# The first norm inside the first block's stream, the second norm beside its tail, and a reordered lead-in of the experts

## The chip, the cores and the metric

The kernel runs on one core of one Trainium2 chip. The metric is the time on the device in microseconds (us) of one execution. "Engines" are TensorE (PE, with its weight load PEld), VectorE (DVE), ScalarE (ACT), GpSimd (POOL) and SyncE (SP), which issues most of the DMAs.

## What is computed

Two blocks on 256 tokens of width 2048, float32. The change touches the first block: a norm, an input projection whose columns go to a gated linear attention (GLA, 4 heads) and to a dilated window attention (12 heads), the output projection with the residual, a second norm, and an expert layer.

```python
def rms_norm(x, g):
    y = x * lax.rsqrt(jnp.mean(x * x, axis=-1, keepdims=True) + EPS)
    return y * g
...
    xn = rms_norm(x, norm1_g[l])
    h = xn @ w_in[l]
    qa, ka, va, gdf, gdb, ra, qd, kd, vd = jnp.split(h, split_points, axis=-1)
    oa = gla_mixer(qa, ka, va, gdf, gdb, ra, ...)   # gates: log_sigmoid(gd @ up + bias)
    od = dilated_mixer(qd, kd, vd, ...)
    x = x + concatenate([oa, od]) @ w_out[l]
    x = x + peer_ffn(rms_norm(x, norm2_g[l]), w_query, sub_keys, expert_down, expert_up)
```

`peer_ffn` makes 8 query heads, scores each against two sets of 128 keys, takes the best 16 pairs of each head and gathers their rows of `expert_down` and `expert_up` (8 KB each), 128 rows per token: the dot with the normed token through a gelu, times a softmax gate, weighs the up row.

## The kernel before

**Stream.** `project` (L429) runs a list of weight chunks (`Stream`). A chunk is 2 of the 16 row tiles of a weight (512 KB; the two gate chunks hold 8 each, 288 KB). SP loads it into one of 8 slots once the chunk that was there is used, ACT rounds it (`high`, L466), DVE subtracts (`low`, L487), and TensorE does three matmuls for each tile, high by high, high by low and low by high (L517, L520). ACT and DVE run through the chunks ahead of TensorE as far as the slots allow. Finished blocks are taken out by ACT (L412), or, for the output projection `out1`, added to the residual by DVE (L409) and squared by ACT (L419) for the next norm. The activations have high and low parts too; those of the first block are made inside the stream (L394, L399).

**Beside work.** Everything of the attentions lies in generators that run at ticks (two chunks each, written by hand): `gla_beside` (L636) starts with tick 2, where TensorE multiplies the gates (L690), DVE adds the bias (L822) and ACT and DVE make the log gate (L775 to L827), for which TensorE waits at tick 4 (L694). On SP, ACT and DVE a tick comes 3 ticks (6 chunks) earlier in the chunk count than on TensorE. Within one engine the order of the program is the order of the work.

**First norm.** Ahead of the stream `normalise` (L529) waits for x and for all constants (1505 KB), squares (L561, L580), takes the root (L563), the reciprocal (L586), scales x (L566, L589), turns it on TensorE (L607) and takes it out with the gain (L569, L592). The weights of the first eight chunks are loaded meanwhile.

**Second norm.** The same function runs between the stream and the experts, with the squares' sums from the stream (L578).

**Experts.** `peer` (L1208): queries (L1287), with those of head 0 split by tokens (L1303) and its scores (L1309); DVE sorts (L1475 to L1512); POOL gathers a row for each of 128 tokens (L1459, 2.10 MB) into 4 slots; DVE makes the dot (L1551), ACT gelu, gate and diagonal (L1392 to L1396), TensorE adds (L1318), and frees the slot. 16 units (8 heads by 2 token tiles) of 16 rows each. Queries of heads 0, 1 and 2 come before the first unit, those of 3 to 7 one step per row inside units 1 to 5. `load_query` (L1200) loads 2 MB for each head into one of two rooms.

## Time and profile before

| | us |
|---|---|
| median of 3 runs | 2331.84 (2329.73 to 2332.44) |
| the profiled execution | 2329.87 |
| its span, first to last instruction | 2328.1 |

```profile
span 2328.1 us, 21752 instructions
...
PE 2056.1 (88%) x8141; PEld 1333.8 (57%) x8141; DVE 1299.4 (56%) x2001; ACT 814.3 (35%) x1737; POOL 260.3 (11%) x267
...
PE   6999999997989889977777898899877799999997
...
PEclk9999999999999999989999999999999999999999
DMA  5545556469999999999999999999999656466662
```

The last three lines cut the span into 40 slices of 58 us; a digit is a share in tenths. The first block's stream fills slices 1 to 8, the expert layer slices 8 to 31, where the DMAs are full, and the second block the rest.

### The profile page before, as it was taken

What the parts mean: (1) busy time and instruction counts of PE and PEld (TensorE: products, weight loads), DVE (VectorE), ACT (ScalarE), POOL (GpSimd) and SP (SyncE); (2) the same over time, 40 slices, a digit from 0 to 9 for tenths busy, and PEclk for the clock granted to TensorE, in tenths of its full rate; (3) what the DMA queues carried; (4) which work ended last, traced back from release to release, by engine and by line L of the source; (5) the groups of instructions that cost most, each with busy time, mean ns of one, the idle gap of its engine ahead of it and who ended that gap; (6) DMA issues with size and microseconds to landing.
All of it is one profiled execution on the core that took longest, in us unless ns stands there. A gap on an engine that the chain in (4) does not pass through costs nothing. (4 is left out here: it accounts for less than half of the span.)

```text
span 2328.1 us, 21752 instructions
## 1 busy us (share of the span) xinstructions
PE 2056.1 (88%) x8141; PEld 1333.8 (57%) x8141; DVE 1299.4 (56%) x2001; ACT 814.3 (35%) x1737; POOL 260.3 (11%) x267
## 2 busy tenths in 40 slices
PE   6999999997989889977777898899877799999997
PEld 5878778772444444422323344444322798999886
DVE  5545665445654555545566555556644666475555
ACT  5446564412212212212222322122121655355454
POOL 0000000002121211112112111111211000000000
PEclk9999999999999999989999999999999999999999
DMA  5545556469999999999999999999999656466662
GB/s 211 163 135 164 162 176 209 166 284 429 427 428 428 427 428 427 426 426 414 428 428 428 427 427 424 426 427 425 413 428 405 202 146 187 123 203 200 185 195 80
DMA packets 87513, 729.90 MB, mean 314 GB/s; under 512 B 10192, under 2 KB 10320, under 8 KB 51696
## 3 DMA queue, kind: packets, MB, share of 16 engines
q0 software_dynamic: 36864, 536.89, 54.4%
q1 hardware_dynamic: 50544, 191.63, 25.5%
q8 instruction: 64, 1.05, 0.2%
q14 instruction: 41, 0.34, 0.0%
HBM read 724.28 MB, written 4.19 MB: 313 GB/s over the span
## 5 line engine op out<-in xcount | busy, mean ns | idle before, releaser
L1318 PE MATMUL bank<-ring,work 128*128 128x512 f32 x2048 | 962.9, 614 | 205.9 <-ACT work L1396 202.9
L1551 DVE CUSTOM_DVE_ANT_0 ring<-ring,mix_t 128x2048 f32<-128x2048 f32 x256 | 586.9, 2293 | 551.9 <-DMA ring<-in_peer_rows_dram,work 549.7
L1318 PEld LDWEIGHTS bank<-ring,work 128*128 128x128 f32 x2048 | 374.6, 192 | 726.2 <-issue 380.7
L487 DVE TENSOR_TENSOR ring_r<-ring,ring_r 128x1024 fp32r<-128x1024 f32 (+2 forms) x300 | 334.5, 1145 | 304.5 <-ACT ring_r L466 303.9
L1459 POOL DMA_INDIRECT ring<-in_peer_rows_dram,work x256 | 256.3, 1001 | 1511.8 <-PE bank L1318 965.2
L1392 ACT ACTIVATE work<-work 128x1 f32<-128x1 f32 x256 | 52.4, 205 | 958.9 <-DVE work L1551 958.8
L520 PE MATMUL bank<-ring_r,mix_r 128*128 128x512 f32 (+1 forms) x1184 | 374.6, 391 | 0.0
L466 ACT ACTIVATE ring_r<-ring 128x1024 fp32r<-128x1024 f32 (+2 forms) x300 | 288.5, 992 | 168.4 <-DMA ring<-in_w_out_dram 52.0
L520 PE MATMUL bank<-ring_r,act_r 128*128 128x512 f32 (+1 forms) x736 | 269.1, 387 | 0.0
L520 PEld LDWEIGHTS bank<-ring_r,mix_r 128*128 128x128 f32 x1184 | 220.3, 189 | 42.1 <-issue 1.8
L517 PE MATMUL bank<-mix_r,ring_r 128*128 128x256 f32 (+1 forms) x1216 | 227.4, 289 | 7.7 <-DVE ring_r L487 7.7
L517 PEld LDWEIGHTS bank<-mix_r,ring_r 128*128 128x128 f32 (+1 forms) x1216 | 191.8, 192 | 9.3 <-DVE ring_r L487 8.2
L517 PE MATMUL bank<-act_r,ring_r 128*128 128x256 f32 (+1 forms) x608 | 174.1, 286 | 0.0
L520 PEld LDWEIGHTS bank<-ring_r,act_r 128*128 128x128 f32 x736 | 138.3, 188 | 27.0
L1287 PEld LDWEIGHTS bank<-act_t,h 128*128 128x128 f32 x576 | 109.0, 190 | 60.7 <-issue 51.7
L1287 PE MATMUL bank<-act_t,h 128*128 128x256 f32 x576 | 142.9, 379 | 0.0
L517 PEld LDWEIGHTS bank<-act_r,ring_r 128*128 128x128 f32 (+1 forms) x608 | 116.7, 192 | 0.0
L1396 ACT ACTIVATE work<-const,work 128x128 f32<-128x128 f32 x256 | 103.2, 403 | 8.3
L520 PE MATMUL bank<-ring_r,h_r 128*128 128x512 f32 x288 | 83.2, 394 | 0.9 <-DVE h_r L2612 0.9
L1393 ACT ACTIVATE work<-work 128x1 f32<-128x1 f32 x256 | 76.1, 297 | 8.3
L412 ACT ACTIVATE h<-bank 128x256 f32<-128x256 f32 (+3 forms) x67 | 32.0, 487 | 123.2 <-PE bank L520 89.1
L520 PEld LDWEIGHTS bank<-ring_r,h_r 128*128 128x128 f32 x288 | 53.8, 188 | 12.6 <-DVE h_r L2612 1.3
(372 smaller groups left out, 1252.1 us busy)
## 6 DMA issues: line engine op xcount, KB each, us to landing
ring<-in_w_in_dil_dram SPq DMA_DIRECT2D x72, 512.0 KB, 3.6
ring<-in_w_out_dram SPq DMA_DIRECT2D x64, 512.0 KB, 3.6
ring<-in_w_in_mo_dram SPq DMA_DIRECT2D x48, 384.0 KB, 3.6
h<-in_w_query_dram SPq DMA_DIRECT2D x8, 2048.0 KB, 11.8
ring<-in_w_in_gla_dram SPq DMA_DIRECT2D x24, 512.0 KB, 3.6
ring<-in_w_in_ml_oz_dram SPq DMA_DIRECT2D x24, 512.0 KB, 3.8
h<-in_xa_wkv_dram SPq DMA_DIRECT2D x4, 2048.0 KB, 21.3
ring<-in_w_in_lru_dram SPq DMA_DIRECT2D x16, 512.0 KB, 3.6
```

Source lines behind the costliest of these rows:

```text
L412: eng.activation(job.dest(c.b, g), src, ACT.Copy).then_inc(k.group_out[False], 1)
L466: act.activation(high(c), raw(c), ACT.Copy).then_inc(k.weights_high, 1)
L487: dve.tensor_tensor(low(c), raw(c), plain(high(c)), ALU.subtract).then_inc(k.weights_low, 1)
L517: m = pe.matmul(bank[0:job.m, 0:T], w[:, q, g * job.m:(g + 1) * job.m], a[:, q, :], start=start, stop=stop)
L520: m = pe.matmul(bank[:, 0:job.cols], a[:, q, g * P:(g + 1) * P], w[:, q, :], start=start, stop=stop)
L1287: m = pe.matmul(bank[:, f * T:(f + 1) * T], a, w, start=kc == 0, stop=kc == KC - 1)
L1318: m = pe.matmul(B[c][:, :], diag[:, d % 2, :], slots[:, d % DEPTH, 1, c * 512:(c + 1) * 512], start=first, stop=last)
L1392: step(act.activation(gelu[:, p, j:j + 1], dots[:, p, j:j + 1], ACT.Gelu_apprx_tanh))
L1393: step(act.activation(coef[:, p, j:j + 1], gelu[:, p, j:j + 1], ACT.Copy, scale=gates[:, p, j:j + 1]))
L1396: act.activation(diag[:, d % 2, :], k.c("ident"), ACT.Copy, scale=coef[:, p, j:j + 1]).then_inc(diag_ready, 1)
L1459: pool.indirect_dma_start(slots[:, d % DEPTH, :, :].rearrange("p a b -> p (a b)"), None, ins["peer_rows"], bass.IndirectOffsetOnAxis(ap=ro ...
L1551: dve.tensor_tensor_reduce(row, row, xn[:, t, :], 1.0, 0.0, ALU.mult, ALU.add, dots[:, p, j:j + 1]) \
```

## The change

- The first `normalise` goes. `norm1_beside` does its work at the head of the stream: a first part of the constants (identity and the gains, 208 of the columns) and x in four pieces of 512 columns are loaded first; TensorE turns x unscaled, two pieces at tick 0 and two at tick 0.5, that is behind the first gate chunk; ACT takes out the high part with the gain and DVE the low part; the squares follow at ticks -1.5 to 0, mean and root at 0.5, the reciprocal at 1. The root `rstd1` is applied where the blocks are taken out (ACT's scale) and, for the gates, in the bias step. The other constants are loaded at tick -1, and `gla_beside` waits for them. L394 and L399 fall away.
- The parts of `out1`'s activations change places: high in `mix_r`, low in `act_r` and `mix_r`.
- The second `normalise` goes. `norm2_beside` turns the unscaled residual, quarters 0 and 1 inside the stream's last chunks, quarters 2 and 3 behind it; ACT and DVE take out two pieces of each quarter; the root goes to the scores' take-outs (`staged`, `later`).
- In `peer` there are three rooms for queries (the third in `mem_kv` and the gain's place), each load is two DMAs of 1 MB, head 2 is loaded once the gain is used and its query moves into unit 0; score 0 and score 1 come after 6 of 16 matmuls of the next group; `xn` is made by one product of x, root and gain.

The diff, cut:

```diff
+                scale = 1.0 if job.scale is None else job.scale[:, g:g + 1]
+                eng.activation(job.dest(c.b, g), src, ACT.Copy, scale=scale).then_inc(k.group_out[False], 1)
...
+def norm1_beside(k, mem, beside, stream, name="norm1"):
+    B, gain, ins = k.banks, k.c("norm1_g"), k.ins
+    x_hi, x_lo = shaped(k.mix_r[:, :], KC, T), shaped(k.act_r[:, :], KC, T)
+    junk = shaped(k.h[:, 0:NT * D], NT, 4, 512)
+    ident_in, const_in, x_turned, x_high, x_low, squared_act, squared_dve, own, meaned, rooted, inverted = (
+        k.sem(f"{name}_{n}") for n in ("ident_in", "const_in", "x_turned", "x_high", "x_low", "squared_act", "squared_dve",
+                                       "own", "meaned", "rooted", "inverted"))
+    x_in = [k.sem(f"{name}_x_in{b}") for b in range(4)]
+    cols = lambda b: slice(b * 512, (b + 1) * 512)
+    turn_at = lambda kc: B[(4, 5, 6, 7, 2, 3, 4, 5)[kc // 2]][:, kc % 2 * T:(kc % 2 + 1) * T]
+    TICKS = (-AHEAD, -AHEAD, -AHEAD + 0.5, -AHEAD + 0.5)
+    SQUARES = [-AHEAD + 1.5 + 0.5 * b for b in range(4)]
+    x_rows = ins["x"].rearrange("(t p) d -> p t d", p=P)
+    def load(sp):
+        yield -AHEAD
+        sp.dma_start(k.const[:, 0:FIRST_CONSTS], ins["consts"][:, 0:FIRST_CONSTS]).then_inc(ident_in, 16)
+        for b in range(4):
+            if b == 2:
+                yield TICKS[b]
+            sp.dma_start(k.x3[:, :, cols(b)], x_rows[:, :, cols(b)]).then_inc(x_in[b], 16)
+        yield -AHEAD + 2
+        sp.dma_start(k.const[:, FIRST_CONSTS:], ins["consts"][:, FIRST_CONSTS:]).then_inc(const_in, 16)
+    def tensor(pe):
+        yield 0
+        pe.wait_ge(ident_in, 16)
+        for b in range(4):
+            if b == 2:
+                yield 0.5
+            pe.wait_ge(x_in[b], 16)
+            if b == 3:
+                pe.wait_ge(x_low, 4)
+            for kc in range(4 * b, 4 * b + 4):
+                for t in range(NT):
+                    m = pe.transpose(turn_at(kc)[:, t * P:(t + 1) * P], k.x3[:, t, kc * P:(kc + 1) * P], k.c("ident"))
+                if kc % 2:
+                    m.then_inc(x_turned, 1)
+    def scalar(act):
+        for b, tick in enumerate(TICKS):
+            yield tick
+            if b == 0:
+                act.wait_ge(ident_in, 16)
+            for kc in range(4 * b, 4 * b + 4):
+                act.wait_ge(x_turned, kc // 2 + 1)
+                act.activation(x_hi[:, kc, :], turn_at(kc), ACT.Copy, scale=gain[:, kc:kc + 1]).then_inc(x_high, 1)
+        for b, tick in enumerate(SQUARES):
+            yield tick
+            act.wait_ge(x_in[b], 16)
+            act.activation(junk[:, 0, b, :], k.x3[:, 0, cols(b)], ACT.Square, accum_out=k.sums3[:, 0, b:b + 1]).then_inc(squared_act, 1)
+        yield 0.5
+        act.wait_ge(meaned, 1)
+        act.activation(mem.sd1, mem.ms1, ACT.Sqrt).then_inc(rooted, 1)
+        yield 3
+        act.wait_ge(inverted, 1)
+    def vector(dve):
+        for b, tick in enumerate(TICKS):
+            yield tick
+            for kc in range(4 * b, 4 * b + 4):
+                dve.wait_ge(x_high, kc // 2 * 2 + 2)
+                dve.scalar_tensor_tensor(x_lo[:, kc, :], turn_at(kc), gain[:, kc:kc + 1], x_hi[:, kc, :].bitcast(F32),
+                                         ALU.mult, ALU.subtract).then_inc(x_low, 1)
+        for b, tick in enumerate(SQUARES):
+            yield tick
+            dve.wait_ge(x_in[b], 16)
+            x = k.x3[:, 1, cols(b)]
+            dve.tensor_tensor_reduce(junk[:, 1, b, :], x, x, 1.0, 0.0, ALU.mult, ALU.add, k.sums3[:, 1, b:b + 1]).then_inc(squared_dve, 1)
+        yield 0.5
+        dve.wait_ge(squared_act, 4)
+        dve.wait_ge(squared_dve, 4)
+        dve.tensor_reduce(mem.sd1, k.sums3, AX.X, ALU.add).then_inc(own, 1)
+        dve.wait_ge(own, 1)
+        dve.tensor_scalar(mem.ms1, mem.sd1, 1.0 / D, EPS, ALU.mult, ALU.add).then_inc(meaned, 1)
+        yield 1
+        dve.wait_ge(rooted, 1)
+        dve.reciprocal(mem.rstd1, mem.sd1).then_inc(inverted, 1)
+        dve.wait_ge(inverted, 1)
+    beside.load.append(load)
+    beside.tensor.append(tensor)
+    beside.scalar.append(scalar)
+    beside.vector.append(vector)
+    for n in range(2):
+        stream.chunks[n].needs = [(x_low, KC // 2 * (n + 1))]
+    return const_in
...
-            step(dve.tensor_tensor(la[:, t, :], B[4 + t][:, :], bias, ALU.add))
+            step(dve.scalar_tensor_tensor(la[:, t, :], B[4 + t][:, :], mem.rstd1[:, t:t + 1], bias, ALU.mult, ALU.add))
...
+def norm2_beside(k, mem, beside, stream, out1, rstd, name="norm2"):
+    B, gain = k.banks, k.c("norm2_g")
+    turned, taken_act, taken_dve, own, meaned, rooted, inverted = (k.sem(f"{name}_{n}") for n in (
+        "turned", "taken_act", "taken_dve", "own", "meaned", "rooted", "inverted"))
+    first, end = stream.at(out1, 2), len(stream.chunks)
+    TICKS = [(first + 5) / PER_TICK, (first + 6) / PER_TICK, end / PER_TICK, end / PER_TICK + 1]
+    turn_at = lambda kc: B[kc // 2 % 4][:, kc % 2 * T:(kc % 2 + 1) * T]
+    def tensor(pe):
+        for b, tick in enumerate(TICKS):
+            yield tick
+            pe.wait_ge(*stream.out(out1, b))
+            if b >= 2:
+                pe.wait_ge(taken_act, 2 * (b - 1))
+                pe.wait_ge(taken_dve, 2 * (b - 1))
+            for kc in range(4 * b, 4 * b + 4):
+                for t in range(NT):
+                    m = pe.transpose(turn_at(kc)[:, t * P:(t + 1) * P], k.x3[:, t, kc * P:(kc + 1) * P], k.c("ident"))
+                if kc % 2:
+                    m.then_inc(turned, 1)
+    def scalar(act):
+        for b, tick in enumerate(TICKS):
+            yield tick
+            if b == 3:
+                act.wait_ge(meaned, 1)
+                act.activation(mem.sd, mem.ms, ACT.Sqrt).then_inc(rooted, 1)
+            act.wait_ge(turned, 2 * b + 1)
+            for kc in (4 * b, 4 * b + 1):
+                act.activation(k.act3[:, kc, :], turn_at(kc), ACT.Copy, scale=gain[:, kc:kc + 1]).then_inc(taken_act, 1)
+    def vector(dve):
+        for b, tick in enumerate(TICKS):
+            yield tick
+            dve.wait_ge(turned, 2 * b + 2)
+            for kc in (4 * b + 2, 4 * b + 3):
+                dve.tensor_scalar(k.act3[:, kc, :], turn_at(kc), gain[:, kc:kc + 1], None, ALU.mult).then_inc(taken_dve, 1)
+            if b == 2:
+                dve.wait_ge(k.squared, NT * 4)
+                dve.tensor_reduce(mem.sd, k.sums3, AX.X, ALU.add).then_inc(own, 1)
+                dve.wait_ge(own, 1)
+                dve.tensor_scalar(mem.ms, mem.sd, 1.0 / D, EPS, ALU.mult, ALU.add).then_inc(meaned, 1)
+        dve.wait_ge(rooted, 1)
+        dve.reciprocal(rstd, mem.sd).then_inc(inverted, 1)
+    beside.tensor.append(tensor)
+    beside.scalar.append(scalar)
+    beside.vector.append(vector)
...
+    gla.scale = dil.scale = mem.rstd1
...
-    def load_x(sp, arrived):
-        sp.dma_start(k.x3, ins["x"].rearrange("(t p) d -> p t d", p=P)).then_inc(arrived, 16)
-        sp.dma_start(k.const[:, :], ins["consts"]).then_inc(arrived, 16)
-    normalise(k, "norm1", k.x3, k.c("norm1_g"), k.act3, load=load_x, upcoming=stream)
     beside = Beside()
-    gla_turned, gla_low = gla_beside(k, mem, beside, stream.out(gates, 0), *(stream.out(gla, b) for b in range(3)))
+    const_in = norm1_beside(k, mem, beside, stream)
...
+def query_room(head):
+    if head < 3:
+        return head, 1
+    return (0, (head + 1) // 2) if head % 2 else (1, head // 2)
+def query_before(head):
+    return head - 3 if head < 5 else head - 2
...
-            for head in range(2, PEER_H):
-                sp.wait_ge(query_done, head - 1)
+            sp.wait_ge(gained, NT)
+            load_query(sp, k, 2, query_in)
+            for head in range(3, PEER_H):
+                sp.wait_ge(query_done, query_before(head) + 1)
                 load_query(sp, k, head, query_in)
...
-            for f in range(2):
-                first_tokens(f, 0, B[4 + f][:, 0:P]).then_inc(first_query, 1)
+            pe.wait_ge(*query_there(0))
+            first_tokens(0, 0, B[4][:, 0:P]).then_inc(first_query, 1)
+            first_tokens(1, 0, B[5][:, 0:P], range(6))
             pe.wait_ge(keys_in, 16)
             first_score(0)
-            first_tokens(0, 1, B[0][:, 0:P])
+            first_tokens(1, 0, B[5][:, 0:P], range(6, KC)).then_inc(first_query, 1)
+            first_tokens(0, 1, B[0][:, 0:P], range(6))
             first_score(1)
+            first_tokens(0, 1, B[0][:, 0:P], range(6, KC))
...
-            query(2, 0, range(KC))
-            score(2, 0)
             for n in range(UNITS):
                 for j in range(K):
-                    if 0 < n < PEER_H - 2:
+                    if n < PEER_H - 2:
                         query(n + 2, n % 2, [j])
...
-                dve.tensor_tensor(xn[:, t, :], xn[:, t, :], gain, ALU.mult).then_inc(gained, 1)
+                dve.scalar_tensor_tensor(xn[:, t, :], k.x3[:, t, :], rstd[:, t:t + 1], gain, ALU.mult, ALU.mult).then_inc(gained, 1)
```

## Rows read from the trace of the kernel before

**Rows 1.** Busy us by stretch; last three: granted clock, DMA share, GB/s.
```profile
350.00:400.00 50.00, 50.00 (x231) 41.59 (x230) 28.86 (x41) 25.43 (x43) 0.00 (x0) 1.00 0.56 174
700.00:800.00 100.00, 89.50 (x243) 43.63 (x242) 53.48 (x80) 25.06 (x71) 20.71 (x20) 1.00 1.01 428
```

**Rows 2.** Timeline of the start: start us, busy us, instruction, [idle before <-releaser].
```profile
12.04 2.29 DVE L580 CUSTOM_DVE_ANT_0 mix_t<-x_res 128x2048 f32<-128x2048 f32 x1 [12.04 <-DMA const<-in_consts_dram]
...
16.35 5.39 PE L607 MATMUL bank<-const,mix_t 128*128 128x128 f32 x32 [16.35 <-ACT mix_t L566]
17.20 0.46 ACT L569 ACTIVATE act_t<-bank,const 128x256 f32<-128x256 f32 x1
...
25.60 0.46 PE L517 MATMUL bank<-mix_r,ring_r 128*72 128x256 f32 x2 [3.86 <-DVE ring_r L487]
...
29.53 4.63 DVE L487 TENSOR_TENSOR ring_r<-ring,ring_r 128x1024 fp32r<-128x1024 f32 x4
...
32.83 0.63 PE L520 MATMUL bank<-ring_r,mix_r 128*128 128x512 f32 x2
```

**Rows 3.** DMA issues, 0 to 50 us: KB each, us from issue to landing.
```profile
x_res<-in_x_dram SPq DMA_DIRECT2D x1, 2048.0 KB, 7.7
```

**Rows 4.** Busy time by stretch, at the start (last three: clock, DMA share, GB/s).
```profile
4.00:6.00 2.00, 0.00 (x0) 0.00 (x0) 0.00 (x0) 0.00 (x0) 0.00 (x0) 1.00 1.00 422
...
27.00:28.00 1.00, 1.00 (x6) 1.00 (x5) 1.00 (x2) 1.00 (x2) 0.00 (x0) 0.50 0.00 0
```

**Rows 5.** Timeline of the gate chain, of eight transposes, and of the second norm.
```profile
39.61 0.69 DVE L822 TENSOR_TENSOR x_res<-bank,mem_kv 128x512 f32<-128x512 f32 x1 [0.59 <-PE bank L690]
...
43.53 1.28 ACT L777 ACT_TABLE_LOAD   x1
44.83 1.06 ACT L777 ACTIVATE x_res<-x_res 128x1024 f32<-128x1024 f32 x1
...
49.15 1.22 DVE L827 SCALAR_TENSOR_TENSOR x_res<-x_res 128x1024 f32<-128x1024 f32 x1
...
51.30 0.59 PE L694 MATMUL bank<-x_res,const 128*128 128x256 f32 x2
...
186.96 1.09 PE L1011 MATMUL bank<-const,h 128*128 128x128 f32 x8 [0.75 <-DVE h L967]
...
451.46 1.30 DVE L409 TENSOR_TENSOR x_res<-bank,x_res 128x512 f32<-128x512 f32 x2 [1.42 <-PE bank L520]
...
453.33 0.19 ACT L419 ACTIVATION_READ_ACCUMULATOR work<-x_res 128x1 f32 x1
...
460.42 1.36 DVE L592 TENSOR_SCALAR act_t<-bank,const 128x256 f32<-128x256 f32 x3 [0.30 <-PE bank L607]
...
462.10 7.38 PE L1303 MATMUL bank<-act_t,h 128*128 128x128 f32 x64 [0.84 <-PEq L545]
```

**Rows 6.** Timeline of the experts' lead-in, and one gather of the steady stretch.
```profile
473.11 0.39 PE L1309 MATMUL bank<-h 128*128 128x128 f32 x2
...
477.11 31.05 SPq L1204 DMA_DIRECT2D h<-in_w_query_dram  x3
...
478.10 13.98 PE L1287 MATMUL bank<-act_t,h 128*128 128x256 f32 x64
...
483.34 1.08 POOL L1459 DMA_INDIRECT ring<-in_peer_rows_dram,work  x1 [458.99 <-DVE work L1512]
...
511.32 15.70 PE L1318 MATMUL bank<-ring,work 128*128 128x512 f32 x32 [1.68 <-ACT work L1396]
...
517.49 0.94 POOL L1459 DMA_INDIRECT ring<-in_peer_rows_dram,work  x1 [29.34 <-PE bank L1318]
...
559.23 0.94 POOL L1459 DMA_INDIRECT ring<-in_peer_rows_dram,work  x1 [3.95 <-PE bank L1318]
```

**Rows 7.** Busy time by stretch, around the first gathers.
```profile
480.00:485.00 5.00, 5.00 (x24) 4.39 (x24) 2.32 (x6) 0.00 (x0) 1.36 (x2) 1.00 0.76 321
...
515.00:520.00 5.00, 5.00 (x14) 2.13 (x13) 4.96 (x7) 0.96 (x4) 0.94 (x1) 1.00 0.29 66
```

More of the change, by code:

```diff
@@ L109 @@
 GATE_M = 72
+FIRST_CONSTS = P + 5 * KC
 class Area:
@@ L526, in _, with normalise @@
             rest(len(chunks) // PER_TICK)
-def normalise(k, name, src3, gain, dst3, load=None, upcoming=None, late=None, summed=False):
+def normalise(k, name, src3, gain, dst3, upcoming=None, late=None):
     nc = k.nc
@@ L547, in _ @@
         def _(sp):
-            if load is not None:
-                load(sp, arrived)
             if upcoming is not None:
@@ L596, in _ @@
         def _(pe):
-            if load is not None:
-                pe.wait_ge(arrived, 32)
             for kc in range(KC):
@@ L628, in __init__ @@
         self.top, self.den = area.take(DIL_H, NT), area.take(2, DIL_H, NT)
+        self.ms1, self.sd1, self.rstd1 = (area.take(NT) for _ in range(3))
         area = Area(x[:, :])
@@ L1299, in score, with first_tokens @@
                 m.then_inc(scored, 1)
-            def first_tokens(f, t, bank):
-                for kc in range(KC):
-                    m = pe.matmul(bank, wq[:, 0, kc, f * PEER_K:(f + 1) * PEER_K], k.act3[:, kc, t * P:(t + 1) * P],
+            def first_tokens(f, t, bank, part=range(KC)):
+                for kc in part:
+                    m = pe.matmul(bank, wq(0, kc)[:, f * PEER_K:(f + 1) * PEER_K], k.act3[:, kc, t * P:(t + 1) * P],
                                   start=kc == 0, stop=kc == KC - 1)
```

112 lines of the change are left out of this document (62 added, 50 removed).

## The prediction

> **What bounds the kernel now.** I read first the stretches by busy time and granted clock, to see which engine has no room. In the first block's stream TensorE is busy 50 of 50 us at the full clock, with the DMAs at half load [rows 1]: there every microsecond by which the stream starts earlier should arrive at its end. In the expert stage it is the other way round: the DMAs are at 1.01 and 428 GB/s while TensorE is busy 89.5 of 100 [rows 1], and the 2.10 MB of one gather take 4.9 us at that rate. There the time is that of the bytes, plus the holes in which the DMAs idle. So four places count: the norm ahead of the stream, the seam between stream and expert stage, the lead-in to the first gathers, and the bytes and holes behind it. The timelines of these are what I read next.
>
> **Part 1, the first norm.** Before, nothing starts until x and all constants have landed at 12.04 [rows 2], though x's own transfer, the first one, issued at about 0.75, took 7.7 us [rows 3]; the first gate matmul starts at 25.60 and the first one of the tok chunks at 32.83 [rows 2]. I work the change out in the order in which each engine has it. The DMAs run at 422 GB/s from 4 us on [rows 4], and x as a whole was in by 8.45 [rows 3]; counted back at that rate, the small constants and the first quarter of x, 0.63 MB together, are in at about 4.9, the second quarter at 6.2, the rest by 9.4. TensorE turns the first quarter. Before, the first copy followed the first transpose by 0.85 us with two transposes [rows 2]; with four, 1.1: 6.1. ACT takes 8 pieces at 0.45 each (0.46 alone [rows 2]): 9.7. It rounds the gate weights and DVE subtracts (0.67 and 0.75): the first gate chunk can start at 11.1. The other half's transposes stand behind that chunk in TensorE's order. The granted clock was 0.50 (1.2 GHz) in the stretch from 27 us [rows 4], about 1 us after TensorE had come back from a wait of 3.86 us, and full again at about 30. Here the wait is 3.5 us, so I take the chunk slow. Sixteen steps took 7.1 us with that drop [rows 2]; eight take 2.8 fast and 4.2 with one. That gives 15.3. Eight more copies from 16.0 end at 19.6, rounding and subtraction at 21.0, the second gate chunk with a drop again at 25.2 (22.6 at the full clock). So TensorE comes to the tok chunks 7.6 us earlier (up to 10).
>
> Not all of that stays. The squares on ACT (0.62 each) and DVE (0.65 each), the mean and the root now lie in the same programs as the rounding of the weights. DVE subtracts a chunk in 1.14 (four took 4.63 [rows 2]). It begins chunk 2 at 21.1; eight chunks (9.1), four squares (2.6) and the steps between the engines for mean, root and reciprocal (2.3) put it at 35.1 for the gate logits, which TensorE has ready at 32.8. Before, DVE began them at 39.61, the log gate was ready at 50.37, and TensorE came for it at 51.30, 0.9 us later [rows 5]. From logits to log gate are 10.8 us, two weight chunks among them: 35.1 + 10.8 = 45.9. TensorE, coming at 43.7, waits 2.2 us. **What is late next** is thus this chain over DVE and ACT. Gain at that point 51.3 - 46.0 = 5.3; with one more drop of the clock behind the wait 3.6; with no drop anywhere 6.7. I take **4.5 us**, ends 1 and 9 (no row shows x in pieces of 2 KB a partition; a later landing goes one to one).
>
> The root needs a table on ACT where before that was loaded in the empty start. A load takes 1.28 us, and the next ACTIVATE starts 0.02 behind it [rows 5]; it falls in the wait for the mean and costs at most 1. The Trainium skill ("ScalarE: Activation LUTs", What ACT_TABLE_LOAD costs) adds a drain of 1.38 us to each load. By it the log gate would come about 1 us later. The trace shows no such drain.
>
> The scale at the take-outs lengthens ACT copies, where ACT is busy 25.4 of 50 us [rows 1]: nothing. The second part of the constants, 1.4 MB, lands at about 15 and its first reader comes at 30: nothing. SP's four small loads no longer stand behind the norm: nothing, their readers are later.
>
> **Part 2, the second norm.** Before, TensorE ends the stream at 452.0, the last take-out at 452.76, the squares at 453.52, the norm's last take-out at 461.78, and the queries start at 462.10 [rows 5]. After, half of the 32 transposes lie inside the stream, which TensorE bounds; eight in a row took 1.09 us with their tail [rows 5], 0.117 apart: +1.9 us. Sixteen are left behind it: TensorE turns the third quarter until 453.0, the fourth until 454.0; ACT ends its squares, copies two pieces until 454.4, takes the root at 454.85 and copies two more until 455.95; DVE ends with the reciprocal at 456.0. With the 0.32 us that the change of programs took, the queries start at 456.3: 5.8 earlier, less 1.9 is 3.9. But TensorE then sat idle for 2.3 us. Waits of 3.86 and 1.68 us [rows 2, 6] were followed by a drop of the clock, one of 0.84 us [rows 5] was not; a drop costs about 1.7 (half of 3.4). I take it: **2.2 us**, ends 1 and 4.
>
> **Part 3, the lead-in.** Call the queries' start S (462.10 before). Score 1 starts at S+11.0 and the first gather at S+21.24 [rows 6]. After, 16 + 6 matmuls, score 0, 10 + 6 matmuls and then score 1: 38 steps of 0.231 and 0.22, S+9.0. The first gather is issued 2.0 us earlier against S. DVE's new product of x, root and gain (two of about 2.4) ends at S+4.8, ahead of the first sort at S+5.9. Query 2 and its score leave the lead-in and are spread over the first unit, as the later ones are. The first added row, at S+49.2 before [rows 6], now needs query 1 (S+16 to S+30, 13.98 long [rows 6]), its take-out and the gate's exponential (S+32.4), the normalised gate (33.0), the first dot (2.4: 35.4) and the diagonal: S+36.4.
>
> **Part 4, bytes and holes.** The end is decided by the DMAs. At S+15 the load of head 2 was issued [rows 6]; from there the DMAs are nearly full to the last gather, with two holes: at 321 GB/s from 480 to 485, 1.2 us lost ahead of the first gather, and at 66 GB/s from 515 to 520, 4.2 us lost [rows 7], where the four slots were full and no row had been added yet; the fifth gather is issued at 517.49 [rows 6]. After, head 2 goes into a third room from S+5 on, while the DMAs are idle, and at S+15 it is head 3. One load less lies behind S+15: **4.9 us**, the gather period [rows 6]. The Trainium skill ("DMA: Bandwidth & Descriptors", Where 436 GB/s comes from) says that reads from HBM are held to about 358 GB/s; by that this load would be worth 5.9 us. The trace has 428 over 100 us [rows 1]. The first hole is filled by the earlier gather: **1.2**. The second: head 3, four rows and head 4, six transfers of 4.9 from S+17, keep the DMAs until S+46.4. The first row is added from S+36.4 to S+42.3 (5.9 us, as long as before with the half clock), so the fifth gather is issued at S+42.6, some 2 us before it is needed with its latency. From there TensorE takes 3.43 + 0.87 = 4.3 us a row, under 4.9. So the hole closes: **4.2**, ends 0 and 4.2. Together 10.3; I take **9.9**, ends 6 and 11.
>
> **The sum**: 4.5 + 2.2 + 9.9 = 16.6 us. The profiled execution took 2329.87 (span 2328.10), 2 us under the median of the runs, 2331.84; it would be 2313.3, the median 2315.
>
> **Rivals.** (a) More: no clock drops, and the log gate not late: 6.7 + 3.9 + 10.9 = 21.5, up to 25 us: 2307 to 2310. For it: the trace has waits with no drop behind them. Against: those over 1.6 us that I looked at had one. (b) Less: the second hole stays, since the first row's chain on ACT (query take-out, gate, two copies, two tables) or the half clock makes it over 4 us late, and x lands late: 2 + 2 + 6 = 10 us, 2322. (c) Only the byte and hole terms come, the stream's earlier start being given back at the log gate: 2321. (d) Slower: the pace of the gathers. Some 252 rows lie behind the hole. If the loads in two pieces of 1 MB, or the queries in the first units, leave the four slots such that a row takes 4.965 us, the 16.6 are gone; from 4.985 on the kernel is over 0.2% slower, 2336.5. Against: TensorE has 0.6 us of room per row, and units with a query kept the full DMA rate [rows 1]. (e) The change doesn't do what it says: the second hole is not TensorE's but lies in the order of the transfers; then it is (b) again.
>
> **Chances.** The forecast (16.6, within 4) 0.52, (a) 0.20, (b), (c) and (e) together 0.20, a gain under 0.2% 0.04, (d) 0.04. The range takes in (a) and most of (b) and (c): 2306.5 to 2323.5. A measurement of this kernel can tell about 0.2%, 4.7 us, from no change: faster 0.9, same 0.06, slower 0.04.
>
> **What would show it.** First gate matmul at 11, first tok chunk at 25, a TensorE wait for the log gate of 2 us near 44; 16 transposes in the stream without a stall; queries at about 455.5; first gather near 474.5; no hole of the DMAs between 475 and 530; the last gather some 16 us earlier and everything behind it as before. A hole behind the fourth row, a wait of over 5 us at the log gate, or a gather period other than 4.9 would make it wrong.

## The result, and the profile after

The changed kernel takes 2315.55 us (median of four runs, 2312.02 to 2316.95) where the kernel before takes 2330.78: ratio 0.9932, 95% interval 0.9915 to 0.9949. The forecast was 2315. Two repeats gave 2317.38 and 2316.64. The gain was thus 15.2 us where 16.6 were forecast, and 12.6 and 14.1 in the repeats: the forecast time came out so close partly because the kernel before, with a fourth run, has a median 1.1 us below the 2331.84 that the forecast started from. The profiled execution of the changed kernel took 2312.02, which is also its fastest; between the two traces lie 17.9 us, 2.6 more than between the medians. I therefore compare places in the traces rather than whole spans.

The page of the changed kernel (span; busy time by engine; DMA share by slice, in tenths):

```profile
span 2310.2 us, 21761 instructions
...
PE 2053.5 (89%) x8141; PEld 1331.8 (58%) x8141; DVE 1294.7 (56%) x2008; ACT 811.0 (35%) x1743; POOL 265.8 (12%) x267
...
DMA  6545556499999999999999999999998656466662
```

The page hardly differs from that of before: the work is the same to 3 us of TensorE. What moved shows only in the timelines. Its timeline (start us, busy us, engine, line, operation, then idle before and who ended it), from the start to the steady gathers:

```profile
0.76 0.86 SPq L326 DMA_DIRECT2D ring<-in_w_in_gates_dram  x2
1.67 1.85 SPq L326 DMA_DIRECT2D ring<-in_w_in_gla_dram  x4
3.56 0.43 SPq L669 DMA_DIRECT2D const<-in_consts_dram  x1
4.03 3.07 SPq L673 DMA_DIRECT2D x_res<-in_x_dram  x4
...
12.89 3.28 PE L688 MATMUL bank<-const,x_res 128*128 128x128 f32 x16 [12.89 <-DMA x_res<-in_x_dram]
...
18.31 0.46 PE L520 MATMUL bank<-mix_r,ring_r 128*72 128x256 f32 x2 [2.14 <-DVE act_r L715]
...
27.51 0.46 PE L520 MATMUL bank<-mix_r,ring_r 128*72 128x256 f32 x2 [2.88 <-DVE act_r L715]
...
30.39 0.63 PE L523 MATMUL bank<-ring_r,mix_r 128*128 128x512 f32 x2
...
49.06 0.70 PE L790 MATMUL bank<-x_res,const 128*128 128x256 f32 x2
...
451.98 2.04 PE L1261 MATMUL bank<-const,x_res 128*128 128x128 f32 x16
...
454.25 0.20 ACT L1270 ACTIVATE work<-work 128x2 f32<-128x2 f32 x1
...
455.48 5.15 PE L1482 MATMUL bank<-act_t,h 128*128 128x128 f32 x44 [1.47 <-PEq L432]
...
474.84 1.08 POOL L1637 DMA_INDIRECT ring<-in_peer_rows_dram,work  x1 [472.29 <-DVE work L1690]
...
490.56 1.28 ACT L1571 ACT_TABLE_LOAD   x1 [2.02 <-DVE work L1729]
492.87 5.40 PE L1497 MATMUL bank<-ring,work 128*128 128x512 f32 x8 [4.63 <-ACT work L1575]
499.04 0.94 POOL L1637 DMA_INDIRECT ring<-in_peer_rows_dram,work  x1 [19.39 <-PE bank L1497]
```

Three places in it are used throughout. **G** is the first matmul behind the wait for the log gate: 51.30 before [rows 5], 49.06 here. **S** is the queries' start: 462.10 before [rows 5], 455.48 here. **E** is the start of the addition of the last row's sums; it was 1810.30 before and 1792.62 here, both the start of the last such addition, whose row in the changed kernel is

```profile
1792.62 2.48 DVE L1702 TENSOR_TENSOR x_res<-bank,x_res 128x512 f32<-128x512 f32 x4 [4.79 <-PE bank L1497]
```

G moved by 2.2 us, the stretch from G to S went from 410.80 to 406.42 (4.4), and S to E from 1348.2 to 1337.1 (11.1). They add to 17.7 of the 17.9 us by which the span fell, so nothing of note changed behind the experts. Around the first gathers, the stretches by busy time (PE, PEld, DVE, ACT, POOL; last three: granted clock, DMA share, GB/s), which answer to [rows 7]:

```profile
480.00:485.00 5.00, 5.00 (x25) 4.41 (x24) 0.00 (x0) 0.00 (x0) 0.00 (x0) 1.00 0.98 416
515.00:520.00 5.00, 4.56 (x13) 2.19 (x13) 4.09 (x7) 0.90 (x3) 0.96 (x1) 1.00 1.00 429
```

Both holes are gone from these stretches: 416 and 429 GB/s where there were 321 and 66. Since the queries start 6.6 us earlier, the same stretch is another place in the work; the 45 us from S+15 to S+60 (S+15 is 15 us behind S) hold both holes wherever they lie. Before, after, the second trace of the changed kernel, and the kernel with two rooms (both below):

```profile
477.10:522.10 45.00, 41.41 (x169) 31.19 (x170) 19.54 (x53) 9.11 (x22) 5.77 (x6) 0.96 0.86 350
470.48:515.48 45.00, 38.99 (x136) 25.35 (x137) 23.45 (x56) 9.64 (x24) 7.63 (x8) 0.96 0.99 409
472.36:517.36 45.00, 39.14 (x135) 25.41 (x136) 22.50 (x56) 9.64 (x24) 7.84 (x8) 0.92 0.98 397
472.47:517.47 45.00, 39.14 (x135) 25.43 (x136) 22.71 (x56) 9.65 (x24) 7.64 (x8) 0.92 0.98 402
```

Against the full 428 GB/s [rows 1] these 45 us lose 8.2, 2.0, 3.3 and 2.7 us: an estimate from the last column, used again below.

At the start, by contrast, little went as forecast: x is issued behind six weight chunks, and the first gate matmul starts at 18.31 where I had 11.1.

### The profile page after: what moved, and what is told of

The parts are those of the page before. It is cut to its first block and busy times, and to the rows that moved or that the text cites. A ratio compares the mean times of both kernels' runs of the same rounds, so it can differ in the third digit from the quotient of the medians.

```text
span 2310.2 us, 21761 instructions
## 1 busy us (share of the span) xinstructions
PE 2053.5 (89%) x8141; PEld 1331.8 (58%) x8141; DVE 1294.7 (56%) x2008; ACT 811.0 (35%) x1743; POOL 265.8 (12%) x267
## 5 line engine op out<-in xcount | busy, mean ns | idle before, releaser
L1637 POOL DMA_INDIRECT ring<-in_peer_rows_dram,work x256 | 261.7, 1022 | 1510.5 <-PE bank L1497 951.0
L523 PE MATMUL bank<-ring_r,mix_r 128*128 128x512 f32 (+1 forms) x1312 | 400.4, 392 | 0.0
L523 PEld LDWEIGHTS bank<-ring_r,mix_r 128*128 128x128 f32 x1312 | 244.3, 189 | 47.0 <-issue 1.0
L523 PE MATMUL bank<-ring_r,act_r 128*128 128x512 f32 (+1 forms) x608 | 234.5, 386 | 0.0
L1466 PEld LDWEIGHTS bank<-act_t,h 128*128 128x128 f32 x544 | 102.9, 190 | 62.8 <-issue 55.0
L1466 PE MATMUL bank<-act_t,h 128*128 128x256 f32 x544 | 137.2, 379 | 0.0
L523 PEld LDWEIGHTS bank<-ring_r,act_r 128*128 128x128 f32 x608 | 114.5, 188 | 22.1
L523 PE MATMUL bank<-ring_r,work_r 128*128 128x512 f32 x192 | 59.8, 392 | 0.0
```

The costliest lines, as they stand in the source:

```text
L523: m = pe.matmul(bank[:, 0:job.cols], a[:, q, g * P:(g + 1) * P], w[:, q, :], start=start, stop=stop)
L1466: m = pe.matmul(bank[:, f * T:(f + 1) * T], a, w, start=kc == 0, stop=kc == KC - 1)
L1637: pool.indirect_dma_start(slots[:, d % DEPTH, :, :].rearrange("p a b -> p (a b)"), None, ins["peer_rows"], bass.IndirectOffsetOnAxis(ap=ro ...
```

## The experiments

The kernel before took 2329.99 beside the first group (the repeat, the start at once, two rooms, the old first norm), 2331.73 beside the second (query 2, turning behind, the old second norm, all of x first), 2330.77 beside the last two; each ratio is to the one beside it. "The repeat" is the first run below; where a kernel of another group is set against it, up to 1.7 us of the difference can be that of the groups, and the places in the traces count.

**The changed kernel again.**

> The changed kernel once more, beside the experiments on the same chip: the base line. Expected as before: span about 2310 to 2315 us, queries (first matmul of head 0) at 455.5, first gather at 474.8, fifth gather at 499.0, last dot 17.7 us earlier than in the kernel before. If the runs differ by some us while these times agree, the difference lies in the steady stretch of the gathers.

Measured: 2317.38 us (2316.1 to 2318.36), ratio 0.9942 (0.9925 to 0.9959). G 50.92, S 457.36, S to E 1340.3. One and the same kernel passes the log gate at 49.06 or at 50.92. Its timeline and two stretches:

```profile
27.83 0.46 PE L520 MATMUL bank<-mix_r,ring_r 128*72 128x256 f32 x2 [2.88 <-DVE act_r L715]
...
32.25 0.62 PE L523 MATMUL bank<-ring_r,mix_r 128*128 128x512 f32 x2
...
50.92 0.70 PE L790 MATMUL bank<-x_res,const 128*128 128x256 f32 x2
...
20.00:21.00 1.00, 1.00 (x7) 1.00 (x6) 0.00 (x0) 0.00 (x0) 0.00 (x0) 1.00 1.00 342
...
30.00:31.00 1.00, 1.00 (x6) 1.00 (x6) 0.21 (x2) 0.00 (x0) 0.00 (x0) 0.50 0.06 16
```

The second gate chunk takes 4.4 us (27.83 to 32.25) at a granted clock of 0.50. In the changed kernel's first trace it took 2.9 (27.51 to 30.39), after the same idle time of 2.88 us. The 1.5 us more at the tok chunk, with the 0.3 before it, are the 1.9 by which G and S are later. The first gate chunk is slow too: in the stretch from 20 us TensorE gets through 7 matmuls, where it gets through 11 in a fast one, yet the row has the full clock. So the granted clock alone does not show every slow stretch.

**The start in the order that the ticks say.** The runner of the beside programs starts each of them at tick 0; everything written with a lower tick runs at tick 0, behind the loads, the roundings and the subtractions of the first six chunks. This kernel lets them start at once:

```diff
     def runner(self, eng, programs):
-        tasks = [[0, program(eng)] for program in programs]
+        tasks = [[-math.inf, program(eng)] for program in programs]
```

> One edit: the runner of the beside work starts its tasks at minus infinity and not at 0, so that the negative ticks of the first norm are what they say: constants and x are issued ahead of the weights, and ACT and DVE take x out ahead of rounding the weights. Theory A (my reading of the changed trace): x landed at 12.9 only because its DMAs were issued behind six weight chunks, since no task runs ahead of tick 0. Then x's first quarter lands at about 5, the first gate matmul is at about 11 (18.3 in the changed kernel), the first tok chunk at about 25 (30.5), and TensorE has to wait about 2 us for the log gate, since eight weight chunks now stand between; it passes it at 46.0 (49.06), 3 us earlier than the changed kernel, total 3 us less (2 to 4). Theory B: x in four pieces of 2 KB a partition is slow by itself, or the DMAs bring nothing earlier; then the first quarter lands at 8 or later and the log gate is passed at 49 as before, total unchanged. Theory C: the log gate's chain over DVE and ACT takes the whole gain: passed at 48 to 49, with a wait of 4 us or more.

Measured: 2314.26 us (2312.24 to 2314.95), ratio 0.9929 (0.9913 to 0.9946). Its timeline:

```profile
0.75 0.39 SPq L669 DMA_DIRECT2D const<-in_consts_dram  x1
1.20 0.94 SPq L673 DMA_DIRECT2D x_res<-in_x_dram  x2
...
5.68 3.71 PE L688 MATMUL bank<-const,x_res 128*128 128x128 f32 x16 [5.68 <-DMA x_res<-in_x_dram]
...
13.05 0.67 PE L520 MATMUL bank<-mix_r,ring_r 128*72 128x256 f32 x2 [3.67 <-DVE ring_r L490]
...
47.05 0.70 PE L790 MATMUL bank<-x_res,const 128*128 128x256 f32 x2 [0.83 <-DVE x_res L924]
```

Constants and x are issued first, x's first quarter is there at 5.68, the tok chunks begin at 27.57, and now TensorE does wait for the log gate, 0.83 us, and passes it at 47.05. G and S (453.53) are 3.9 and 3.8 us earlier than in the repeat beside it, the median is 3.1 lower. So the order of the start that I had worked out exists in this kernel, and not in the one I was to forecast.

**Two rooms for the query weights.** One part of the change is undone: heads 0 and 1 alone are loaded early, head 2 as before.

```diff
 def query_room(head):
-    if head < 3:
-        return head, 1
-    return (0, (head + 1) // 2) if head % 2 else (1, head // 2)
+    return head % 2, head // 2 + 1
 ...
-    return head - 3 if head < 5 else head - 2
+    return head - 2
 ...
-            sp.wait_ge(gained, NT)
-            load_query(sp, k, 2, query_in)
-            for head in range(3, PEER_H):
+            for head in range(2, PEER_H):
 ...
```

> The changed kernel with two rooms for the queries, as before: head 2 is loaded once query 0 is done (about 15 us behind the queries' start) and no longer at 5 us; its query stays inside unit 0. The byte term alone. Theory A (bytes decide): one load of 2.10 MB more lies in the stretch in which the DMAs are full, the end moves back by 4.9 us, no hole appears. Theory B (the row's chain decides, bytes are hidden): nothing changes, within 1 us. Theory C: the two-room order makes unit 0 wait for head 2 or 3, a hole of over 2 us between 480 and 530 and 7 us or more.

Measured: 2320.36 us (2318.11 to 2321.2), ratio 0.9953 (0.9937 to 0.997), 3.0 above the repeat. S 457.47, as the repeat, and S to E 1344.1. Its last addition:

```profile
1801.57 2.48 DVE L1699 TENSOR_TENSOR x_res<-bank,x_res 128x512 f32<-128x512 f32 x4 [4.79 <-PE bank L1494]
```

Over all nine profiled executions with the changed order of the lead-in and three rooms, S to E has a mean of 1339.7 (1337.1 to 1341.5). Against that, this kernel is 4.4 us longer, near the 4.9 of one load; against before (1348.2) it is 4.1 us shorter. Both are single traces, and the nine spread over 4.4 us, so by themselves these two differences are good to some 2 us. The rates say more: between S+15 and S+60 this kernel loses 5.5 us less than the one before, against 5.4 for the two holes in the forecast.

**The first norm as before.** The first norm stands ahead of the stream again, with x and constants whole; all else as changed.

```diff
-            step(dve.scalar_tensor_tensor(la[:, t, :], B[4 + t][:, :], mem.rstd1[:, t:t + 1], bias, ALU.mult, ALU.add))
+            step(dve.tensor_tensor(la[:, t, :], B[4 + t][:, :], bias, ALU.add))
 ...
-    gla.scale = dil.scale = mem.rstd1
 ...
+    normalise_old(k, "norm1", k.x3, k.c("norm1_g"), k.act3, load=load_x, upcoming=stream)
     beside = Beside()
-    const_in = norm1_beside(k, mem, beside, stream)
 ...
```

> The changed kernel with the first norm as it was, ahead of the stream (all else as changed, the constants' order too). Theory A: the new place of the first norm is worth what the log gate shows, 2.2 us (49.06 against 51.30), and this is carried through the stream: everything from there on is 2.2 us later than in the changed kernel, total 2.2 us more (1.5 to 3). Theory B: it is given back in later waits of the stream: queries' start within 0.5 us of the changed kernel.

Measured: 2317.2 us (2316.6 to 2320.75), ratio 0.9948 (0.9931 to 0.9964), within 0.2 of the repeat beside it. Its timeline:

```profile
51.46 0.59 PE L874 MATMUL bank<-x_res,const 128*128 128x256 f32 x2
...
457.11 5.15 PE L1568 MATMUL bank<-act_t,h 128*128 128x128 f32 x44 [1.47 <-PEq L432]
```

S is 457.11; in the kernels that have both norms as changed (two of them with another lead-in, which lies behind S) it is 455.48, 456.11, 456.20, 457.36 and 457.47. The first norm's move, as it was written, is worth between nothing and 1.6 us at S, 0.6 in the mean of these five. And from G to S are 405.65 us here against 410.80 before: the second norm alone brings 5.15.

**Query 2 ahead of the first unit.** Query 2 and its score go back into the lead-in, ahead of the first row; the early load stays.

```diff
             score(1, 1)
+            query(2, 0, range(KC))
+            score(2, 0)
             for n in range(UNITS):
                 for j in range(K):
-                    if n < PEER_H - 2:
+                    if 0 < n < PEER_H - 2:
 ...
```

> The changed kernel with query 2 and its score back ahead of the first unit; the third room and its early load stay. It prices the hole of the DMAs. Theory A (the first added row frees the first slot, and the DMAs run dry before it): the fifth gather moves from 44 to about 55 us behind the queries' start, while the DMAs have only six transfers of 4.9 us, until 46 or 47; a hole of 8 to 10 us appears, twice that of the kernel before, since one load less fills it; total 8 to 10 us more than the changed kernel. Theory B (the hole was in the order of the transfers and not TensorE's): under 2 us more. Theory C: the faster rows of unit 0 (no query steps in them) make up for half: 4 to 5 us.

Measured: 2326.74 us (2324.4 to 2330.75), ratio 0.9984 (0.9975 to 0.9994). S 456.11, S to E 1350.3, 10.6 more than the mean of the others. A row of its timeline, and two stretches (last three columns: granted clock, DMA share, GB/s):

```profile
509.98 2.07 POOL L1640 DMA_INDIRECT ring<-in_peer_rows_dram,work  x1 [29.69 <-PE bank L1497]
...
505.00:510.00 5.00, 4.50 (x11) 2.11 (x12) 4.66 (x11) 1.32 (x5) 0.02 (x1) 1.00 0.00 0
510.00:515.00 5.00, 5.00 (x13) 2.17 (x12) 4.86 (x11) 1.80 (x6) 3.45 (x2) 1.00 0.49 157
```

The fifth gather is issued 53.9 us after S (43.6 in the changed kernel), and POOL is released by the matmul that added the first row. For 5 us the DMAs move nothing; from S+15 to S+60 they run at 308 GB/s, which loses 12.6 us, some 10 more than in the changed kernel. The hole is set by TensorE's order: one query and its score ahead of the first row cost two thirds of the whole gain. It is larger than the one before (8.2); that the load of head 2, which then kept the DMAs busy behind S+15, is now done earlier accounts for it, but I didn't test that apart.

**All of the second norm's turning behind the stream.**

```diff
-    TICKS = [(first + 5) / PER_TICK, (first + 6) / PER_TICK, end / PER_TICK, end / PER_TICK + 1]
+    TICKS = [end / PER_TICK, end / PER_TICK, end / PER_TICK, end / PER_TICK + 1]
```

> The changed kernel with all four quarters of the second norm's transposes behind the stream, none in it. Theory A (as the prediction costed it): the stream ends 1.9 us earlier; behind it the 32 transposes and 16 take-outs, eight on each of ACT and DVE at 0.41 us, end about 1.7 us later, so that the queries start at the same time within 0.5 us, total unchanged: the place of the first two quarters is worth nothing, and what part 2 gains comes from turning unscaled and from the missing change of programs. Theory B: take-outs behind the stream wait for each other's banks and TensorE's clock drops; queries 2 to 4 us later. Theory C: transposes inside the stream cost more than their own 1.9 us, then it is faster by 1 or more.

Measured: 2316.46 us (2314.49 to 2318.45), ratio 0.9934 (0.9918 to 0.9951). Its timeline:

```profile
452.39 1.91 PE L1261 MATMUL bank<-const,x_res 128*128 128x128 f32 x16
...
458.39 5.15 PE L1482 MATMUL bank<-act_t,h 128*128 128x128 f32 x44 [1.58 <-PEq L432]
```

From G to S it takes 407.15 us against 406.44 in the repeat: counted from G, the stream's end comes 1.8 earlier and the queries 0.7 later, and the median doesn't show it. That two quarters are turned inside the stream brings at most 0.7 us. The gain of this part is in what is common to both: turning without waiting for the root, transposes in long runs, and no change of program between them. Which of these three brings how much isn't shown.

**The second norm as before.** `norm2_beside` is taken out, `normalise` runs between stream and experts, the root's scale at the take-outs goes.

```diff
-    norm2_beside(k, mem, beside, stream, out1, rstd)
 ...
+    normalise_old(k, "norm2", k.x3, k.c("norm2_g"), k.act3, summed=True)
     return query_in, keys_in, gain_in
 ...
```

> The changed kernel with the second norm as it was (own program behind the stream, scaled x is turned, gain product without the root), the lead-in and the first norm as changed. Theory A (by the changed trace): part 2 is worth 4.4 us and not 2.2, since TensorE was idle 1.47 us and its clock didn't drop; with the norm before, the stream ends 2 us earlier and the queries start 6.6 us after the last take-out's time more, net 4.4 us later, and all behind it shifts by that. Theory B (2.2, the value of the prediction). Theory C: given back in the lead-in, since the gain product no longer carries the root and the clock stands differently: under 1.

Measured: 2322.84 us (2320.52 to 2323.42), ratio 0.9962 (0.9948 to 0.9976), 5.5 above the repeat, which is of the other group. S 462.10 with G 49.50: 412.60 between them, 6.2 more than in the repeat and 1.8 more than before. The row of the queries, and one stretch:

```profile
462.10 5.15 PE L1567 MATMUL bank<-act_t,h 128*128 128x128 f32 x44 [0.84 <-PEq L619]
...
455.00:460.00 5.00, 5.00 (x26) 5.00 (x25) 2.42 (x5) 3.25 (x7) 0.00 (x0) 0.50 0.00 0
```

The 32 transposes, which go in the pace of their copies, run at half the clock through the whole of this stretch; the granted clock was 0.50 in the old norm of the kernel before too, from 457 to 460. The norm beside the stream had no stretch at 0.50 at the seam in any of its ten traces.

**All of x turned ahead of the first gate chunk.** The start at once, and both halves of x turned in one run.

```diff
-    TICKS = (-AHEAD, -AHEAD, -AHEAD + 0.5, -AHEAD + 0.5)
+    TICKS = (-AHEAD, -AHEAD, -AHEAD, -AHEAD)
 ...
         for b in range(4):
-            if b == 2:
-                yield 0.5
             pe.wait_ge(x_in[b], 16)
```

> The negative ticks honoured, as in e1_ticks, and all sixteen pieces of x turned and taken out ahead of the first gate chunk (all of x is loaded first). Theory A (after e1_ticks the head of the stream is bound by the detour of x's second half over TensorE's first gate chunk): ACT takes 16 pieces in a row until about 14, the gate chunks follow from 16, the first tok chunk at about 22 (27.6 in e1_ticks), the log gate is passed at 42 to 43 (47.05), total 4 to 5 us less than e1_ticks, some 8 less than the changed kernel. Theory B (the chain over DVE and ACT from the squares to the log gate is the bound already, TensorE waited 0.83 us for it in e1_ticks): the first tok chunk is early, but the wait for the log gate grows to 3 us or more; gain over e1_ticks under 2. Theory C: the transposes are bound by x's landing at 9.4 or later, then 2 to 3.

Measured: 2309.44 us (2308.74 to 2311.71), ratio 0.9909 (0.9892 to 0.9925), 5 below the start at once and 8 below the repeat, both of the other group; against the kernel before beside each, it gains 22.3 us where the start at once gains 15.7. Its timeline:

```profile
6.88 1.28 ACT L697 ACT_TABLE_LOAD   x1 [6.88 <-PE bank L686]
8.18 5.94 ACT L697 ACTIVATE mix_r<-bank,const 128x256 fp32r<-128x256 f32 x16
...
16.22 0.43 PE L520 MATMUL bank<-mix_r,ring_r 128*72 128x256 f32 x2 [4.30 <-DVE ring_r L490]
...
23.40 0.63 PE L523 MATMUL bank<-ring_r,mix_r 128*128 128x512 f32 x2
...
42.08 0.70 PE L788 MATMUL bank<-x_res,const 128*128 128x256 f32 x2
```

One wait in place of two: the gate chunks follow each other, the tok chunks begin at 23.40 (27.57 with two), the log gate is passed at 42.08. S is at 448.62, 4.9 earlier than with the start at once (453.53), S to E 1340.5. In the changed kernel's order the second gate chunk waited for a round trip over ACT (eight copies, rounding) and DVE (subtraction) of its own.

**The changed kernel a third time.**

> The changed kernel a third time, as the base line of e8_table_and_constants on the same chip. From the seven executions with the changed first norm so far, the log gate was passed at 49.1 to 51.2 us, by where TensorE's clock dropped among the two gate chunks: a value in this range again, the queries 406.4 us after it, and the sums of the last row 1337 to 1341 us after the queries' start.

Measured: 2316.64 us (2316.0 to 2317.26), ratio 0.9939 (0.9922 to 0.9956). G 49.83, S 456.20, S to E 1341.5.

**Table and constants.** The kernel with all of x first, and a dummy root on ACT while it waits for x, so that the table is loaded in the empty start, and the constants' second part issued later.

```diff
-        yield -AHEAD + 2
+        yield 0
         sp.dma_start(k.const[:, FIRST_CONSTS:], ins["consts"][:, FIRST_CONSTS:]).then_inc(const_in, 16)
 ...
             if b == 0:
                 act.wait_ge(ident_in, 16)
+                act.activation(k.sums[:, NT * 4:NT * 4 + 1], k.c("ident")[:, 0:1], ACT.Sqrt)
```

> e7_all_first with two more edits at its head: a one-element square root on ACT once the identity is in, so that the table for it is loaded in the empty start (in e7_all_first the load of 1.28 us stood at 6.88, between the first turned piece and its take-out, and another one at 24.94 before the root), and the second part of the constants issued behind six weight chunks and not behind four (ACT waited for a weight chunk behind it). Theory A: the first take-out starts at 6.9 (8.18), the gate chunks at 15 (16.2), the log gate is passed 1 to 1.5 us earlier than in e7_all_first, at about 40.8 (42.08), total about 2308. Theory B: the head is bound by x's landing and the clock's drops, then under 0.5 us.

Measured: 2308.46 us (2306.82 to 2308.9), ratio 0.9904 (0.9887 to 0.992). Its timeline and one stretch:

```profile
6.88 6.44 ACT L698 ACTIVATE mix_r<-bank,const 128x256 fp32r<-128x256 f32 x16 [3.88 <-PE bank L686]
...
15.20 0.67 PE L520 MATMUL bank<-mix_r,ring_r 128*72 128x256 f32 x2 [3.43 <-DVE ring_r L490]
...
42.06 0.70 PE L789 MATMUL bank<-x_res,const 128*128 128x256 f32 x2
...
16.00:18.00 2.00, 2.00 (x11) 2.00 (x10) 2.00 (x4) 2.00 (x5) 0.00 (x0) 0.50 1.03 432
```

The copies start 1.3 us earlier and the gate chunks 1.0, but G is where it was (42.06 against 42.08): the chunks run longer at 0.50, and the microsecond is spent before the tok chunks. The median is 1.0 lower, within the two kernels' spreads, and each is 22.3 below the kernel before beside it; so no gain of this edit is shown. It has the lowest median of all that I ran, some 8 us below the changed kernel, of which nearly all is the order of the start.

## Why the forecast held, step by step

The time was met to 0.6 us, and the mechanisms of two parts of three; that the sum fits so well is luck, for two terms were wrong and cancelled. The forecast was the sum 4.5 + 2.2 + 9.9 = 16.6. The means of the changed kernel's three traces against the one of before are 1.4 us (G), 4.4 (G to S) and 8.6 (S to E), together 14.3, and the gains of its three medians have a mean of 14.0.

**Part 1 (4.5 forecast, 2.2 at G in the changed kernel's first trace, 1.4 in the mean of three; 0 to 1.6 at S against the kernel with the old first norm).** The failed step is the very first one, "the small constants and the first quarter of x are in at about 4.9". I took the order of issue from the ticks written in the change (x at -AHEAD; "are loaded first" in the description of the change is wrong in the same way) and didn't follow them through the runner, whose tasks start at 0. So SP issues six weight chunks (0.76 and 1.67) ahead of the constants (3.56) and x (4.03), x's first quarter is there at 12.89, and ACT rounds the same six chunks ahead of the first copy. The gate matmul came at 18.31 instead of 11.1, the tok chunks at 30.39 instead of 25.2, the log gate at 49.06 instead of 46.0, and "TensorE waits 2.2 us" there did not occur. With the order that I had assumed, the start at once gave 5.68, 13.05, 27.57, a wait of 0.83 us and 47.05: that chain was right in kind and 1.0 us too early at its end. It was 2.4 us too early at the tok chunks and had the wait 1.4 too long, which nearly cancel. The first copy came at 8.14 where I had 6.1: x's quarter came 0.8 later, and ACT loaded a table for 1.28 us ahead of that copy, as in the rows of the kernel with all of x first. I had counted a table for the root alone. (The sixteen steps with one drop took 7.2 us, 25.60 to 32.83, and not 7.1.) My ends of 1 and 9 covered it, as "a later landing goes one to one". It did not go one to one: the landing was 8 us late (12.9 against 4.9) and G 3, since the rounding and subtraction of the first chunks were already done by then.

The slow pace at the gate chunks was there, as forecast, but at no fixed place: on the first chunk in the first trace, on both in the second, on the second alone in the third (granted clock 0.50 from 29 to 31 us), and G at 49.06, 50.92 and 49.83. These 1.9 us are nearly as much as this part brought at best.

**Part 2 (2.2 forecast, 5.2 to 6.2 against the kernels with one old norm; 4.4 from G to S against before in each of the changed kernel's three traces, with the longer stretch named below in it).** The working was 3.9, less 1.7 for a drop of the clock behind an idle TensorE. That is the term that was mis-sized: TensorE was idle for 1.47 us and no drop followed: the queries took 5.15 us for their first 44 matmuls, as with the old norm. The other steps were near: the transposes in the stream cost 1.8 (1.9 forecast), the root came at 454.25 (454.85), the queries started 3.5 us behind the stream's end instead of 4.3. What I had not counted is that the old norm had its own drop, and its transposes took 1.3 us longer in the kernel with the old second norm (6.68) than before (5.38). One more thing went the other way: with the changed first norm the stretch from G to the last matmul of the stream is 0.5 to 0.6 us longer (400.92 and 400.86 in the two kernels with nothing turned inside the stream, 400.34 before), and 0.8 from G to S against the kernel with the old first norm (406.4 against 405.65). It isn't the clock drop near 158 us: the mean granted clock from 150 to 170 us was 0.83 in the changed kernel's first two traces, but 0.91 in the third, as in the kernels with the old first norm, and the third is just as long (406.37). The difference grows little by little over the stream, in part with waits of TensorE for DVE's attention steps that are about 0.1 us longer each. The forecast had put the scale at the take-outs at nothing; whether it is that, I haven't shown.

**Parts 3 and 4 (9.9 forecast, 8.5 in the mean of nine traces, 11.1 in the changed kernel's first trace).** Here the steps held. The first gather came at S+19.36 (S+19.24 forecast), and the gathers' period remained 4.9. The byte term was 4.4 (4.9) by S to E of two rooms. The two holes (5.4 forecast) were 4.1 by S to E, two rooms against before, and 5.5 by the rates from S+15 to S+60. What is left of the difference lies in the steady stretch: from S+60 to S+1300 the DMAs lose, summed over slices of 5 us against 428 GB/s, some 6 us in the trace of before and in the first of the changed kernel, 7.4 with two rooms, and 8.2 and 9.5 in the repeats (estimates). With that the account closes: 4.9 for the load + 6.2 for the holes are the 11.1 of the first trace; for the mean of nine it is 4.9 + 5.5, less 1.9 in the steady stretch. The first row was added from S+37.4, 1.0 later than forecast, ACT having loaded a table (1.28 us at 490.56) once the dot was there and not while it waited; the fifth gather went out at S+43.6 instead of S+42.6, still before S+46.4, up to which the DMAs had work, and the hole closed. Here half of the clock was indeed granted: TensorE waited for 4.63 us and the row took 5.40, and 6.17 and 6.52 in the repeats, where 397 and 398 GB/s in the 45 us leave 1.2 to 1.3 us more of the hole.

**The rivals.** (a), more and without drops, was ruled out for the changed kernel by the slow gate chunks and the slow first row, though its 3.9 for part 2 was nearer than the forecast's 2.2; its time, 2307 to 2310, is that of the kernels with a better start. Its sum takes 10.9 for parts 3 and 4, whose terms add up to 10.3. (b) and (e), a hole that stays or that lies in the transfers' order, fell with 429 GB/s at 515 to 520 and with query 2 put back, which opened it again. (c), only the byte and hole terms, fell at S, 4.7 to 6.6 us earlier in all three traces. (d), the gathers' pace, fell with a period of 4.9. The range held all three medians of the changed kernel.

On the rule named in the forecast, "DMA: Bandwidth & Descriptors" of the Trainium skill (Where 436 GB/s comes from), that reads from HBM are held to about 358 GB/s: the traces after do not agree either, 416 and 429 GB/s in the rows above. And on "ScalarE: Activation LUTs" of the Trainium skill (What ACT_TABLE_LOAD costs), a drain of 1.38 us to each load: in the kernel with all of x first the load starts at 6.88 and the copies at 8.18, 1.28 + 0.02 us, so the load of 1.28 agrees and no drain shows.

## What to carry to other kernels

Where a change gives its order by ticks or priorities, follow one of them through the code that runs them before working out a time: the order as written and the order as issued differed here, and with it the largest part of what the first norm could bring. When a chain needs several pieces of an input, one wait for all of them may beat two shorter ones: turning x in two runs rather than one cost 5 us here. For a memory bound stage read where the transfers stop, and ask which engine's order lets the next one go; the queries' order on TensorE was worth 10.6 us there (with the early load in place), more than both norms together.

## What was not expected of the hardware

- The half clock does not follow from the idle time alone. The same kernel had the second gate chunk at 0.50 in one execution and not in the other, behind the same 2.88 us of idle time (4.4 and 2.9 us long). Behind the 1.46 to 1.58 us at the seam no trace had a drop (the first 44 matmuls of the queries took 5.15 us in each); behind 4.63 us the first row took 5.40 to 6.64, where the next one takes 3.60. A drop whose place changes from run to run belongs into the range rather than into the sum; the one at the first row came in every trace with that wait.
- A stretch can be slow at a full granted clock: the first gate chunk of the repeat (7 matmuls in the microsecond from 20 us at 1.00).
- A start of the chunks that is 1 us earlier was taken back by the clock (15.20 against 16.22, then 42.06 against 42.08).
- What is left between executions of one kernel, 2312 to 2318 us, has two sources in these traces: 1.9 us at the gate chunks, and 4.4 us (1337.1 to 1341.5) between the queries' start and the last row. By the DMA rates some 1.2 of the second lie ahead of S+60, where the first row is slower, and the rest in dips of the rate in the steady stretch (6 us lost there in one trace, 8.2 and 9.5 in the others). What makes these dips I have not shown.
